# Two block stacks on one core: the last up side by seven products, and the next weights' sums behind c22

## The reference

```python
# first stack, in each layer
f = (jax.nn.silu(x @ w_gate[l]) * (x @ w_up[l])) @ w_down[l]
x = _layernorm(ALPHA * x + f, ln2_g[l], ln2_b[l])
...
# second stack, in each layer, twice
h = x + 0.5 * swiglu(rms_norm(x, ffn1_norm[l]), ffn1_gate[l], ffn1_up[l], ffn1_down[l])
```

## Time and profile before

| what | value |
|---|---|
| median of three runs | 3070.16 us (3069.99 to 3070.50) |
| the profiled execution | 3071.58 us, of which its span is 3069.8 us |
| TensorE busy | 3041.6 us, 99% |
| VectorE busy | 2007.8 us, 65% |
| GpSimd busy | 1485.1 us, 48% |
| ScalarE busy | 1072.3 us, 35% |
| granted TensorE clock | 0.998 of full speed |

### The profile page before, as it was taken

How to read it: one execution, slowest core, us unless ns; L and a number is a source line. 1 busy time by engine, 2 the same in 40 slices (tenths; PEclk the granted TensorE clock), 3 DMA queues, 4 the chain that set the end, 5 groups by cost and what they waited for, 6 DMA issues and landing times.

```text
span 3069.8 us, 50768 instructions
## 1 busy us (share of the span) xinstructions
PE 3041.6 (99%) x18974; PEld 2690.8 (88%) x18974; DVE 2007.8 (65%) x3190; ACT 1072.3 (35%) x1958; POOL 1485.1 (48%) x2023
## 2 busy tenths in 40 slices
PE   8999999999999999999999999999999999999998
PEld 7879998898799988899887789988899887789987
DVE  5576896175768952899527558962699346559942
ACT  4464342054543420544112334420344022334410
POOL 5346107773461076501978371078402977370094
PEclk9999999999999999999999999999999999999999
DMA  5112222231123232232332123223222332122321
GB/s 189 49 42 74 105 109 100 100 104 49 42 76 110 103 103 97 76 110 100 106 114 90 49 83 109 96 104 103 92 100 103 110 108 88 39 100 103 110 101 65
DMA packets 83081, 284.83 MB, mean 93 GB/s; under 512 B 9531, under 2 KB 15068, under 8 KB 82652
## 3 DMA queue, kind: packets, MB, share of 16 engines
q1 hardware_dynamic: 77484, 273.70, 25.6%
q10 hardware_dynamic: 5424, 8.79, 0.8%
HBM read 278.79 MB, written 3.67 MB: 92 GB/s over the span
## 4 chain that ended last, share of the span: by engine, by line
PE 94%; DVE 3%; ACT 2%; issue 1%; DMA 0%; DVEq 0%; ACTq 0%
PE bank_v L607 16%; PE bank_v L609 15%; PE bank_v L608 15%; PE bank_s L885 10%; PE bank_s L887 10%; PE bank_s L886 10%; PE bank_a L607 3%; PE bank_a L609 2%; PE bank_a L608 2%; PE bank_v L1033 1%; PE bank_a L1012 1%; PE bank_s L1173 1%; PE bank_s L1051 1%; PE bank_v L1188 1%; PE bank_s L661 0%
## 5 line engine op out<-in xcount | busy, mean ns | idle before, releaser
L581 POOL TENSOR_TENSOR w_lo<-raw,w_hi 128x512 fp32r<-128x512 f32 x640 | 876.2, 1369 | 51.2
L577 POOL TENSOR_TENSOR zero<-zero 128x1 f32<-128x1 f32 x640 | 209.6, 328 | 560.8 <-PE bank_v L609 409.7
L570 POOL TENSOR_TENSOR zero<-zero 128x1 f32<-128x1 f32 x96 | 21.8, 227 | 940.7 <-DVE s_lo L2283 527.3
L578 POOL CAST w_hi<-raw 128x512 fp32r<-128x512 f32 x640 | 432.2, 675 | 0.0
L607 PE MATMUL bank_v<-h_hi,w_hi 128*128 128x512 f32 (+1 forms) x1122 | 422.9, 377 | 0.0
L608 PE MATMUL bank_v<-h_lo,w_hi 128*128 128x512 f32 (+1 forms) x1122 | 422.4, 376 | 0.0
L609 PE MATMUL bank_v<-h_hi,w_lo 128*128 128x512 f32 (+1 forms) x1122 | 422.4, 376 | 0.0
L607 PE MATMUL bank_v<-xn_hi,w_hi 128*128 128x512 f32 (+1 forms) x1008 | 380.1, 377 | 8.5 <-DVE xn_lo L2023 8.5
L609 PE MATMUL bank_v<-xn_hi,w_lo 128*128 128x512 f32 (+1 forms) x1008 | 373.9, 371 | 0.0
L608 PE MATMUL bank_v<-xn_lo,w_hi 128*128 128x512 f32 (+1 forms) x1008 | 373.7, 371 | 0.0
L607 PEld LDWEIGHTS bank_v<-h_hi,w_hi 128*128 128x128 f32 x1122 | 211.1, 188 | 38.8
(11 more groups left out here) (445 smaller groups left out, 7808.5 us busy)
## 6 DMA issues: line engine op xcount, KB each, us to landing
raw<-in_w_stream SPq DMA_DIRECT2D x516, 512.0 KB, 3.3
rope<-in_rope ACTq DMA_DIRECT2D x2, 1024.0 KB, 6.3
da_v<-t_rows ACTq DMA_DIRECT2D x2, 1024.0 KB, 7.6
out<-resid SPq DMA_DIRECT2D x8, 256.0 KB, 2.3
t_rows<-t_row ACTq DMA_DIRECT2D x1, 1536.0 KB, 6.8
resid<-in_x ACTq DMA_DIRECT2D x5, 256.0 KB, 7.6
mla_v<-in_alibi ACTq DMA_DIRECT2D x2, 512.0 KB, 7.5
resid<-in_x SPq DMA_DIRECT2D x3, 256.0 KB, 9.6
```

Of the source, the lines that this page charges most:

```text
L577: pool.tensor_tensor(zero[:, 1:2], zero[:, 0:1], zero[:, 0:1], ALU.add)
L578: pool.tensor_copy(w_hi[:, u, cut], raw[:, u, cut]).then_inc(hi_split.sem, 1)
L581: ins = pool.tensor_tensor(w_lo[:, u, cut], raw[:, u, cut], w_hi[:, u, cut].bitcast(F32), ALU.subtract)
```

## The change

It does five things.

1. The up side of the last pair is made by seven products as well, in all six networks. `UPS_PAIRED` goes, "seven" is part of the loop again, and only the ups of pair zero stay plain. `PAIRED_UNITS` takes in the last up's units, so GpSimd no longer splits them.
2. The next weights' sums (`weight_sums`) stand behind c22 and no longer behind u3, on the gate and on the up side, in every pair of the loop.
3. Making h_lo and h_hi in the last pair gets a new order and new places: `H_ORDER` begins with chunks 16, 17, 19, 18; `H_GATE` puts two behind c11 and one behind c12 of the gate side, `H_UP` eight between the steps of the up side, and eleven stand behind the last product.
4. ScalarE's `h_hi` are made when p7 of the last gate side, and p6, p7, p5 and p4 of the last up side are done.
5. In the first `ffn1` the sums of squares stand ahead of block 6 and no longer of block 3.

```diff
-H_ORDER = (2, 3, 4, 5, 0, 1, *range(6, FC))
-H_AHEAD = dict(u3=2, c22=1, c11=1, c21=0, c12=2)
-H_UPS = (8, 12)
+H_ORDER = (16, 17, 19, 18, 2, 3, 4, 5, 0, 1, 8, 6, 7, *range(9, 16), FC - 1, FC - 2)
+H_GATE = dict(c11=2, c12=1)
+H_UP = dict(u2=2, u3=2, c22=1, c11=2, c21=1)
...
-                side_products(tag, "last", "gate", PAIRED - 1)
-                plain_ups("last")
+                for side in SIDES:
+                    side_products(tag, "last", side, PAIRED - 1)
...
-                project((tag, "gate1", 0), a_bank, inside={3: first_sums})
+                project((tag, "gate1", 0), a_bank, inside={6: first_sums})
...
+            def last_up_side(tag, gate_half):
+                keep_p1((tag, "last", "up"))
+                gate_half("last")
+                hidden_hi_early(tag, "gate", "p3", 3, 1)
+                for ends, n, more in (("p6", 4, 2), ("p7", 6, 2), ("p5", 8, 3), ("p4", 11, FC - 13)):
+                    hidden_hi_early(tag, "up", ends, n, more)
+                for n in range(2):
+                    act.wait_ge(*product.after((tag, "last", n)))
+                    hidden_hi(tag, H_ORDER[FC - 2 + n])
...
                 def behind(name):
-                    if name == "u3" and more:
+                    if name == "c22":
                         weight_sums(tag, at, "up", j + 1)
...
+            def last_up_side(tag, some):
...
+                combine_22(key, of(1, 1), lambda name: some(H_UP[name]))
+                dve.wait_ge(*gated.after((*gate, 0)))
+                dve.wait_ge(*multiplied.after((*key, "p2")))
+                dve.tensor_tensor(of(0, 0), work[:, 0:1, HALVES[0]], bank_11.unsqueeze(1), ALU.mult).then_inc(*up11_read.done((*key, "c11")))
+                some(H_UP["c11"])
+                combine_21(key, of(1, 0))
+                dve.wait_ge(*gated.after((*gate, 1)))
+                dve.wait_ge(*c21_read.after((*key, "c21")))
+                dve.tensor_tensor(of(1), of(1), work[:, 1:2, :], ALU.mult).then_inc(*product.done((tag, "last", 0)))
+                some(H_UP["c21"])
+                combine_12(key, of(0, 1))
+                dve.wait_ge(*c12_read.after((*key, "c12")))
+                dve.tensor_tensor(of(0, 1), of(0, 1), work[:, 0:1, HALVES[1]], ALU.mult).then_inc(*product.done((tag, "last", 1)))
+                some(FC)
...
                     def behind(name):
-                        if name == "u3" and more and at != "zero":
+                        if name == "c22" and more and at != "zero":
                             weight_sums(tag, at, "gate", j + 1)
```

More of the change, by code:

```diff
@@ L70 @@
     for j in range(PAIRED):
-        for side in range(2 if tag in UPS_PAIRED and 0 < j < PAIRED - 1 else 1):
+        for side in range(2 if j else 1):
             PAIRED_UNITS[start + 2 * PLAIN + 4 * j + 2 * side] = len(PAIRED_UNITS)
@@ L903, in side_products @@
                     pe.wait_ge(*c11_read.before((*key, "c11")))
-                    if tag in UPS_PAIRED and at != "zero":
-                        pe.wait_ge(*(up11_read.after((tag, "seven", "up", "c11")) if at == "last" else
+                    if at != "zero":
+                        pe.wait_ge(*(up11_read.after((tag, "pair", "up", "c11")) if at == "last" else
                                      up11_read.before((tag, at, "up", "c11"))))
@@ L1552, in hidden_hi, with hidden_hi_early @@
                 act.activation(h_hi[:, f, :], hidden[:, f, :], ACT.Copy).then_inc(*x_hi.done((tag, "h", f)))
[L1554 to L1558, removed]
+            def hidden_hi_early(tag, side, ends, n, more):
+                act.wait_ge(*multiplied.after((tag, "last", side, ends)))
+                act.wait_ge(*product.after((tag, "pair", 1)))
+                for f in H_ORDER[n:n + more]:
                     hidden_hi(tag, f)
[L1561 to L1565, removed]
+            def last_up_side(tag, gate_half):
[7 more added lines that the diff above has]
+                    hidden_hi(tag, H_ORDER[FC - 2 + n])
             def first_pair_hi(tag):
@@ L1576, in all_pairs @@
                 gate_half("zero")
[L1577 to L1587, removed]
+                first_up_hi(tag)
+                with loop(act, tag, PAIRED - 2) as i:
+                    gate_side("pair", i + 1)
+                    up_side(tag, "pair", i + 1, gate_half)
                 gate_side("last", PAIRED - 1)
-                gate_half("last")
-                hidden_hi_rest(tag)
+                last_up_side(tag, gate_half)
             def ffn(tag):
@@ L2396, in some @@
                         done.append(f)
[L2398 to L2407 removed]
+                return some
             def ffn(tag):
```

91 lines of the change are left out of this document (28 added, 63 removed).

## The result

The changed kernel takes 3115.4 us (median of 4 runs, 3115.1 to 3116.5) where the kernel before takes 3070.3 beside it (3070.0 to 3071.6): a ratio of 1.0147, 95% interval 1.0129 to 1.0164. The forecast was 3105.7 with a range of 3076 to 3114. The direction and the places were right, but the loss is 45.1 us and not 35.5, and the time lies 1.4 us above the range.

A forecast was written before the change was run, and what follows sets the result against it. TensorE, busy 3041.6 of 3069.8 us, was taken as the bound. The terms - 5.0 - 2.7 + 8.4 + 4.1 + 3.1 + 27 + 0.6 gave + 35.5 us, a median of 3105.7, range 3076 to 3114.

The forecast's parts named there:

- Part 1: Last up side by seven products in six networks: 10.07 for 10.91 us each, 5.0 us less on TensorE.
- Part 2: First pairs: with c22 ahead of the sums, TensorE's waits go, 0.42 us per `ffn` call and 1.82 in first `ffn1`.
- Part 3: Steady pairs: VectorE's scaled sides outlast TensorE's, and `ffn` waits on ScalarE's c11: 8.4, 4.1 and 3.1 us more.
- two gaps named: Added to VectorE's scaled side: 0.12 us for c22 directly behind u3, 0.23 us for the low part awaiting ScalarE.
- Part 4: Start of `down`: its first output chunk waits for h_lo slowed by GpSimd, 4.5 us a network, 27 us in six.
- U: Time of the last up side's first product; `down` starts at U + 10.07, h_lo of chunk 15 ends at U + 24.6.
- Part 5: First `ffn1`, moved sum of squares: the ln_sum wait goes, but the sum comes 0.6 us later; 0.6 us more.
- (a): Rival: only `down` pays, the sides absorb the 0.12 and 0.23 us and cost nothing: 3090, chance 0.15.
- (b): Rival: only the sides pay, GpSimd finishes two units early and h_lo cost 0.6 to 0.8 us: 3079, chance 0.12.
- (c): Rival: all cover holds, products are saved, c22's waits go and nothing new waits: 3063, chance 0.11.
- (d): Rival: in between, half of `down`'s loss and nothing else new, within 0.2% of the kernel before: chance 0.04.
- (e): Rival: more than counted, h_lo slowed as by the page's lock between VectorE and GpSimd: 3125, chance 0.05.

The follow-up runs named there:

- E1: The changed kernel with the next weights' sums back behind u3 on both sides of every steady pair: 3095.4 us, 1.0079 of the kernel before.
- E11: The kernel before with the sums behind c22 and the low part of S2 and S3 behind c21 in steady pairs: 3068.8 us, ratio 0.9992.
- E5: The changed kernel with the low part of S4 made on one column of 512 in every steady pair: 3094.8 us, 1.0078 of the kernel before.
- E7: The changed kernel with the low part of S2 and S3 behind c21, not c11, on both sides: 3095.2 us, 1.0079 of the kernel before.
- E3: The changed kernel with GpSimd splitting only 2 of 512 columns in each half of the first four down units: 3083.3 us, 1.0042 of the kernel before.
- E4: The changed kernel with GpSimd waiting before each network's third down unit until h_lo of chunk 9 is made: 3095.5 us, 1.0081 of the kernel before.
- E2: The kernel before with only the sums moved behind c22 in every steady pair, last up units plain: 3088.0 us, ratio 1.0057.

## Why the prediction was right in kind and too small

- *Part 1* (- 5.0 us). Right: 10.07 for 10.91 us in six networks.
- *Part 2* (- 2.7 us). Right: no p3 of a first pair waits for c22 in the two `ffn` calls, and in the first `ffn1` that wait, 1.3 us in E1, is gone (the 0.7 left in the list is in its gate side zero). But the 1.82 us there don't go whole: VectorE still comes late, p1 of the up side waits 0.4 us for c11, and even E11 takes only 0.88 us off that stretch. Part 3 had put 1.34 us of that lateness back.
- *Part 3* (+ 15.6 us). The mechanism was right (E5, E7: a VectorE side longer than TensorE's, by just the two gaps named), the size was short: 22.0 measured. Net of part 2 the sides lost 19.2 and not 12.9 us. The failed step is "A side comes to 9.97 + 0.12 + 0.23 = 10.32 us". It was worked out on a gate side and held there (10.34), but used for both: in the up side c22 starts 0.60 us behind u3 (2281.08 to 2281.68) where the gate side's takes 0.46 (2270.75 to 2271.21), and the up side is 10.47. With 0.40 us over TensorE's side for seven up sides and 0.27 for six gate sides the prediction's sum for a scaled call gives 4.0 us, as measured, and not 2.8. Why c22 takes longer there stays open: it writes a slice of `hidden` that the loop's index selects, but so does the multiplication at 2286.84, which starts 0.44 us behind the c21 that it reads. In `ffn`, the 3.1 became 4.7: TensorE's side was 0.32 late where I had 0.26, and the next one 0.07 more.
- *Part 4* (+ 27 us). Right in kind (E3, E4) and in pattern: chunk 0, 6, 10, 13 wait, and h_lo take 1.11 us each in the last row of eleven. Measured 31.2 (31.4 by the stretches): 4.8 us in `ffn`, where 4.5 was forecast, and 5.5 in the four scaled calls. The failed step is "With 1.03 each, 17.5 us: 3.07 + 2.2 + 1.85 + 17.5 = U + 24.6", one price of h_lo for all six networks. In `ffn` that held: h_lo of chunk 15 is done at U + 24.9. In the scaled calls it is done at U + 25.5. Their last gate side has two steps more in SBUF, beside GpSimd (one takes 1.47 us for its usual 0.43), and they hold up GpSimd too, whose first two casts take 1.1 us there and 0.61 in `ffn`. The views are VectorE's and GpSimd's timelines, of a scaled call and then of `ffn`:

```profile
2400.03 1.47 DVE L2454 TENSOR_TENSOR work<-work,scale_by 128x256 f32<-128x256 f32 x1
2402.56 0.42 DVE L2281 TENSOR_TENSOR parts<-parts,bank_s 128x256 f32<-128x256 f32 x1 [0.45 <-PE bank_s L887]
2402.90 1.61 DVE L2382 TENSOR_TENSOR h_lo<-hidden,h_hi 128x512 fp32r<-128x512 f32 x1
...
2402.66 1.30 POOL L581 TENSOR_TENSOR w_lo<-raw,w_hi 128x512 fp32r<-128x512 f32 x1
```

```profile
495.69 1.51 DVE L2382 TENSOR_TENSOR h_lo<-hidden,h_hi 128x512 fp32r<-128x512 f32 x2
...
494.75 1.30 POOL L581 TENSOR_TENSOR w_lo<-raw,w_hi 128x512 fp32r<-128x512 f32 x1
```

  u2 starts 3.18 us into the side in both, with idle time ahead of it, so VectorE isn't late there. But GpSimd's low part begins 3.28 us into the side and not 2.59, and the h_lo behind u2 meets nearly all of it: two h_lo take 1.43 us from there to u3 in `ffn` and 2.13 in the scaled call. u3 starts 5.65 us into the side and not 4.96, and all behind it is 0.7 late. This is read off the timelines; E3, where the last side takes 10.06 us in all six networks, shows that it goes with GpSimd's work. Four calls of 0.7 are 2.8 of the 4.2 us that were missing; the rest is of the size of the 0.26 us between U + 24.6 and U + 24.86 in each network.
- *Part 5* (+ 0.6 us). Wrong in mechanism, small in size. The wait for ln_sum is gone, but TensorE now waits 1.1 us for w_lo of GpSimd in the plain up ahead of the first gate side (the list above). From the end of `ffn`'s second `down` to the first gate side of `ffn1` it is 58.22 us for 58.17: a wait changed its name.
- *The rivals.* (a), only `down` pays, and (b), only the sides pay, fell with E1 and E2, each of which shows one of the two losses alone. (c) and (d) fall with both. (e), in which VectorE and GpSimd exclude each other for whole steps, has h_lo at 1.30 us: the row of eleven has 1.11. Its 3125 also doesn't go with the "some 23 us more" worked out ahead of it, which would be 3129.
- The sum as measured: - 5.0 + 19.2 + 31.2 + 0.05 - 1.4 = + 44.0, where the spans differ by 43.8. The - 1.4 is below. The upper bounds of the parts (14 and 5 for part 3, 33 for part 4, 0.7 for part 5) add up to 3115.2, so the range, which ended at 3114, was closed under its own bounds. The scaled calls and the first `ffn1` together lost 17.3 us in the sides, over their bound of 14; part 3 in `ffn`, part 4 and part 5 stayed within theirs.

## What to carry to other kernels

When two engines run at the same pace to within 1 or 2%, work out what a moved step costs on every variant of the loop body (each side, each call), since a tenth of a microsecond a side adds up over the calls. A step put between another and its reader can be worth more than the place that is argued about: here that gave back the 20 us that the move had cost. Work taken off the bottleneck engine only pays if the partner engines' last burst in front of the next stage still fits, with their contention counted.

## What the runs showed of the hardware

- VectorE's steps with two SBUF inputs and GpSimd's go in turns: in the steady state of the first `down` chunk GpSimd makes one half unit in 3.31 us, and three h_lo stand in it, of 0.68, 1.09 and 1.77 us. The Trainium skill ("SBUF — State Buffer", Who interferes with whom) has the two exclude each other. The trace agrees on who is slowed: h_lo starts every 1.11 us and not 0.60, and GpSimd's cast takes 1.08 us and not 0.61. It doesn't agree with a full exclusion, since part of GpSimd's time is open to VectorE: a half unit alone takes 2.1 us (517.27 to 519.35 in E4), and beside it three h_lo of 0.6 lose only 1.5. The timeline of GpSimd:

```profile
508.19 0.64 POOL L577 TENSOR_TENSOR zero<-zero 128x1 f32<-128x1 f32 x1
508.76 1.08 POOL L578 CAST w_hi<-raw 128x512 fp32r<-128x512 f32 x1
509.92 1.62 POOL L581 TENSOR_TENSOR w_lo<-raw,w_hi 128x512 fp32r<-128x512 f32 x1
511.50 0.64 POOL L577 TENSOR_TENSOR zero<-zero 128x1 f32<-128x1 f32 x1
```

- Two VectorE steps of 256 columns start 0.33 us apart if they are independent (2271.61 to 2271.94 in E7), and 0.44 to 0.53 if the second reads the first's result (u2 to u3, 2280.64 to 2281.08). c22 of the up sides, which reads u3, takes 0.60, and 0.68 in E7.
- The kernel before has a short fall of the clock in its profile that the changed kernel's hasn't. For 3.4 us from 888.5 on the granted clock is 0.50, its 1.2 GHz level. TensorE isn't idle ahead of it: its last idle time over 0.1 us ended at 845.2, and from 885.1 to 887.7 it makes 24 products of one column (L703). The changed kernel makes the same products and runs on at 1.00. The table of stretches (us, busy us of each engine, granted clock, DMA share, GB/s), of before (16 products in 2.9 of the 3.4 us) and then of after:

```profile
888.90:891.80 2.90, 2.90 (x16) 2.90 (x15) 1.57 (x7) 0.25 (x1) 0.00 (x0) 0.50 0.00 0
```

```profile
894.60:896.30 1.70, 1.70 (x17) 1.70 (x16) 1.17 (x6) 0.10 (x1) 0.00 (x0) 1.00 0.00 0
```

  It costs some 1.4 us: from the end of `ffn`'s first network to the next gate side zero it is 313.0 us before and 311.6 after. Ten of the fourteen profiles have this fall, at 822 to 893 us; all fourteen have one like it at 37 or 278 us. I found nothing in the kernels that sorts them.
